# Query and key rotation by transfers instead of matrix products, a query product moved forward, and small edits at gates, reciprocals and the end

## The chip, the cores and the metric

One core of one Trainium2 chip runs the whole kernel. The metric is the device time of one execution in microseconds (us); the time before is the median of 3 runs. The granted clock of TensorE is 1.00 (2.4 GHz) in nearly the whole span.

## The reference, cut to what matters

512 tokens of width 1024 pass through two blocks of one kind ("block1", depth 2) and one of another kind. All is float32. In a block of the first kind:

```python
h = rms_norm(x, norm_mix_w[i])
proj = jnp.einsum("bld,de->ble", h, w_in[i])
q, k, v, z, xbc_raw, dt_raw = jnp.split(proj, split_at, axis=-1)
q = rms_norm(q.reshape(b, l, 8, 64), q_norm_w[i])
k = rms_norm(k.reshape(b, l, 2, 64), k_norm_w[i])
q = axial_rope(q, cos_r, sin_r, cos_c, sin_c)
k = axial_rope(k, cos_r, sin_r, cos_c, sin_c)
attn_out = blocked_gqa(q, k, v)
ssd_out = ssd_mixer(z, xbc_raw, dt_raw, ...)
x = x + jnp.einsum("ble,ed->bld", jnp.concatenate([attn_out, ssd_out], -1), w_out[i])
```

`axial_rope` splits the 64 channels of a head into a row half and a column half, and each half into two pieces of 16, `x1` and `x2`, and gives `x1*cos - x2*sin` and `x2*cos + x1*sin`. The SSD mixer runs a centred convolution of five taps and a silu over `xbc`, then a chunked scan (4 chunks of 128 tokens, 2 directions), a gate with silu(z) and a group norm. A gated feed-forward layer follows each block. The third block has a recurrence with heads, a gated linear recurrence (`lru`) with a gelu gate, a long convolution, and another feed-forward layer; a last rms norm ends the program.

## The kernel before, in words

**Tiling.** Activations lie with channels on the 128 partitions and the 512 tokens along the free dimension, 8 tiles for a width of 1024. A weight product of one 128-column tile is 8 rows of the contraction. Each float32 operand is split into a high and a low part in fp32r, and a row is three products (lines 1343 to 1345). The weights come as one stream in the order in which they are used: SyncE loads a slot into `WR` (4 buffers, line 2481), ScalarE rounds it to `WHI` (line 1614), VectorE takes the rest as `WLO` (line 1994). Small products (transposes, attention, scan) are plain float32 products and show as two records each for 512 columns.

**Order.** A planner (`class Order`) writes one list of steps before the build; each engine runs its own steps of that list in that order, so an instruction that waits holds up what stands behind it on its engine. The planner keeps a clock of its own: `TIMES` gives an assumed cost per step, a weight product advances the clock, and chains (generators) wait in it until steps are added (`added`) or assumed done (`until`), or until a PSUM bank is free (`room`). A chain's steps are put between the rows of the weight products when they are due.

**block1.** After the z product come the products dt (column 2192), v (640) and then `IN_ORDER` = (4, 10, 11, 12, 13, 14, 15, 0, 1, 2, 3, 16, 17): keys; x (10 to 13) and B (14, 15) for the scan; the four query tiles; C (16, 17). Each of keys and queries is evicted to a slot of `RQ` (line 1696). Every `xbc` tile goes through `conv` (VectorE, line 2083) and a silu after every second one (line 1686). Chains beside the products:

- `rotated(l, t)`, t = 0 for keys, 1 to 4 for queries: `rsq` squares on ScalarE (1707); `rmm` sums them on TensorE (1385); `rroot` gives 1/sqrt on ScalarE (1593, 1594); `rnorm` scales on VectorE (2097); `rturn` multiplies with a constant matrix on TensorE (1395) that exchanges the pieces and changes a sign; for the keys this is done twice, with a plain product (1393) beside it, since each of the two key heads has to stand on both halves of the partitions (`KD`); `rope` takes `x*cos + turned*sin` on VectorE (2109 to 2111). A rotation waits for the one before.
- `attention`: 16 pairs of heads and token chunks (`pair_chunk`), below called attention chunks, four to each query tile; each starts when keys and its query tile are rotated, at least `pace` (4.0 during the products) apart in the planner's clock. A chunk has a product with the keys (`qk`, 1493), two row maxima (2242), two exps (1775), two reciprocals (`nrm`, 2247), two scalings (`prs`, 1781), eight transposes (1305), two evictions (1788), 16 products with v (`pv`, 1508), a cast and a subtraction (1793, 2252).
- `ssd_states` before, and `ssd_decay`, `ssd_scores`, `ssd_rows` after the last silu (the step `xsilu` 7): products for running sums (1442), scores (1432), then per token chunk c: `dec` (1453), `dexp` (1744), `w` (2196), `xc` (2189), `yt` (1473), `ytc` (1753), `yb`, `gyb`, `gsq` (1758), `zout` (2227). The step `ya` on VectorE (2205) starts the gate of a chunk. When chunk 3 is through, the gated result is transposed back (`zT`).
- After that, four products with `w_out` run together: rows 0 to 3 need attention, rows 4 to 7 the transposed scan result.

**lru.** In block 2, `lru_in(j)` runs two products and, for j of at least 2, lets the planner wait until `yl` of j - 2 is added before the gelu eviction. The gate products (`gates`, 1572) wait for a convolution on VectorE (2361).

**The end.** After the last weight product: add to x (2069, 2071), square (1637), add to the accumulator (2015), a product with ones (1379), 1/sqrt (1593, 1594), then the tiles of x are scaled: 5 on VectorE (2035) and 3, whose norm weight ScalarE has multiplied in before (`xweight`), on GpSimd (`xroot`, 2452). SyncE stores each (2503).

```python
    def rotated(self, l, t):
        if t > 0:
            yield from self.until(("rope", l, t - 1, 1 if t == 1 else 0))
        yield self.add("rsq", l, t)
        ...
        yield self.add("rnorm", l, t)
        for i in range(2 if t == 0 else 1):
            ...
            yield self.add("rturn", l, t, i)
            done = self.add("rope", l, t, i)
```

## Time and profile before

| | us |
|---|---|
| runs shown, median of 3 | 2763.72 (2761.19 to 2764.48) |
| the profiled execution's own time | 2760.8 |
| its span | 2758.8 |
| TensorE busy | 2707.8 (98%) |
| VectorE busy | 1524.2 (55%) |
| ScalarE busy | 1150.2 (42%) |
| GpSimd busy | 22.7 (1%) |
| share of TensorE in the chain that ended last | 91% |

A busy TensorE is one with a product in its pipeline; a full stream of weight products starts one every 0.23 us, so a row takes 0.68 us and a product of 8 rows 5.4 us. The window from 45 to 162.7 us is the product stretch of the first block1, 162.7 to 237.3 us its tail, where scan and attention run without weight products but for the last few us. The second block1 has the same two from 664 to 786.4 and from 786.4 to 861.

### The profile page before, as it was taken

The page shows a single profiled execution, that of the slowest core. Times are in us where ns is not written, and L with a number is a line of the kernel's source. Part 1 is how long each engine was busy: PE and PEld are TensorE (multiplying, and loading weights), DVE is VectorE, ACT ScalarE, POOL GpSimd, SP SyncE. Part 2 cuts the span into 40 slices and gives each one's busy share as a digit, 9 for nine tenths or more (in the row PEclk, how much of TensorE's full clock was granted, in tenths as well). Part 3 has the DMA queues.
Part 4 walks back from the last instruction along what each step waited for, and adds up shares of the span by engine and source line. Part 5 has one row for each costly group of instructions (what it writes and reads, how often), then busy time and mean ns, then how long its engine had stood idle before and what let it go on. Part 6 is the DMA issues. An engine that isn't in the chain of part 4 may idle for free.

```text
span 2758.8 us, 33405 instructions
## 1 busy us (share of the span) xinstructions
PE 2707.8 (98%) x13734; PEld 2183.5 (79%) x13734; DVE 1524.2 (55%) x2136; ACT 1150.2 (42%) x1678; POOL 22.7 (1%) x40
## 2 busy tenths in 40 slices
PE   8998999999999999999999999999999999999997
PEld 6767888888767888888888887777777888888886
DVE  5775444345776444344443446878889854544433
ACT  5585322224584322233222234455587452422221
POOL 0000000000000000000000000000000000000000
PEclk9999999999999999999999999999999999999999
DMA  5102323233201332232332342221223322322231
GB/s 207 61 21 69 108 99 100 92 99 135 69 20 64 113 100 97 94 98 93 100 99 94 95 136 92 69 69 62 81 75 105 123 99 92 99 97 95 96 95 62
DMA packets 72071, 253.42 MB, mean 92 GB/s; under 512 B 8304, under 2 KB 9456, under 8 KB 71536
## 3 DMA queue, kind: packets, MB, share of 16 engines
q1 hardware_dynamic: 69408, 238.19, 26.5%
q0 software_dynamic: 2512, 13.11, 1.3%
q8 instruction: 109, 1.79, 0.3%
q14 instruction: 42, 0.34, 0.0%
HBM read 242.87 MB, written 8.39 MB: 91 GB/s over the span
## 4 chain that ended last, share of the span: by engine, by line
PE 91%; ACT 5%; DVE 3%; issue 1%; DMA 0%; SPq 0%; DVEq 0%; ACTq 0%
PE PS L1343 27%; PE PS L1344 27%; PE PS L1345 27%; PE PS L1526 1%; PE PS L1305 1%; PE PS L1363 1%; PE PS L1364 1%; PE PS L1365 1%; PE PS L1493 1%; ACT PT L1788 0%; PE PS L1508 0%; ACT WHI L1614 0%; ACT DE L1744 0%; PE PS L1424 0%; ACT L1604 0%
## 5 line engine op out<-in xcount | busy, mean ns | idle before, releaser
L1343 PE MATMUL PS<-HHI,WHI 128*128 128x512 f32 x2288 | 915.6, 400 | 0.0
L1345 PE MATMUL PS<-HHI,WLO 128*128 128x512 f32 x2288 | 891.6, 390 | 0.0
L1344 PE MATMUL PS<-HLO,WHI 128*128 128x512 f32 x2288 | 891.2, 390 | 0.0
L1994 DVE TENSOR_TENSOR WLO<-WR,WHI 128x1024 fp32r<-128x1024 f32 (+2 forms) x446 | 536.3, 1204 | 555.8 <-ACT WHI L1614 552.3
L1614 ACT CAST WHI<-WR 128x1024 fp32r<-128x1024 f32 (+2 forms) x446 | 457.4, 1026 | 349.1 <-PE PS L1345 332.5
L1343 PEld LDWEIGHTS PS<-HHI,WHI 128*128 128x128 f32 x2288 | 429.6, 188 | 97.6 <-issue 8.8
L1344 PEld LDWEIGHTS PS<-HLO,WHI 128*128 128x128 f32 x2288 | 429.9, 188 | 92.1 <-issue 7.0
L1345 PEld LDWEIGHTS PS<-HHI,WLO 128*128 128x128 f32 x2288 | 429.5, 188 | 89.9
L1343 PE MATMUL PS<-FHI,WHI 128*128 128x512 f32 x704 | 273.9, 389 | 0.0
L1344 PE MATMUL PS<-FLO,WHI 128*128 128x512 f32 x704 | 273.9, 389 | 0.0
L1345 PE MATMUL PS<-FHI,WLO 128*128 128x512 f32 x704 | 273.9, 389 | 0.0
L1670 ACT CAST FHI<-SQF 128x512 fp32r<-128x512 f32 x88 | 54.6, 620 | 330.3 <-DVE SQF L2055 330.3
L1666 ACT ACTIVATE SQF<-SQF 128x512 f32<-128x512 f32 x88 | 55.6, 632 | 313.9 <-DVE SQF L2048 313.9
L2354 DVE SCALAR_TENSOR_TENSOR CVA<-CU,VEC,CVA 128x511 f32<-128x511 f32 (+14 forms) x240 | 163.6, 728 | 1.9 <-ACT CVA L1886 1.9
L1343 PEld LDWEIGHTS PS<-FHI,WHI 128*128 128x128 f32 x704 | 132.2, 188 | 27.6
L1345 PEld LDWEIGHTS PS<-FHI,WLO 128*128 128x128 f32 x704 | 132.2, 188 | 27.5
L1344 PEld LDWEIGHTS PS<-FLO,WHI 128*128 128x128 f32 x704 | 132.2, 188 | 27.1
L2055 DVE TENSOR_TENSOR SQF<-SQF,PS 128x512 f32<-128x512 f32 x88 | 60.5, 688 | 164.8 <-PE PS L1345 162.0
L2048 DVE TENSOR_TENSOR SQF<-PS,RS 128x512 f32<-128x512 f32 x88 | 60.8, 691 | 142.8 <-PE PS L1345 142.8
L1343 PE MATMUL PS<-YHI,WHI 128*128 128x512 f32 x320 | 127.8, 399 | 2.1 <-DVE WLO L1994 2.1
L1345 PE MATMUL PS<-YHI,WLO 128*128 128x512 f32 x320 | 124.7, 390 | 0.0
L1344 PE MATMUL PS<-YLO,WHI 128*128 128x512 f32 x320 | 124.5, 389 | 0.0
(329 smaller groups left out, 2555.5 us busy)
## 6 DMA issues: line engine op xcount, KB each, us to landing
WR<-in_stream SPq DMA_DIRECT2D x413, 512.0 KB, 3.4
WR<-in_stream SPq DMA_DIRECT2D x32, 384.0 KB, 3.1
xkeep<-X POOLq DMA_DIRECT2D x3, 2048.0 KB, 8.8
X<-xkeep POOLq DMA_DIRECT2D x24, 256.0 KB, 5.0
X<-in_xin SPq DMA_DIRECT2D x8, 256.0 KB, 7.4
out<-X SPq DMA_DIRECT2D x8, 256.0 KB, 2.1
GW<-in_gates SPq DMA_DIRECT2D x8, 128.0 KB, 3.4
RT<-in_rope SPq DMA_DIRECT2D x2, 320.0 KB, 5.6
```

The costliest lines, as they stand in the source:

```text
L1305: t = e.transpose(out[:, i * P:(i + 1) * P], src, ident)
L1343: e.matmul(out, hi[:, i, :], xhi, start=first, stop=False)
L1344: e.matmul(out, hi[:, i, :], xlo, start=False, stop=False)
L1345: t = e.matmul(out, lo[:, i, :], xhi, start=False, stop=final)
L1363: e.matmul(out, xhi, hi[:, i, :], start=r == 0, stop=False)
L1614: e.copy(hi, raw).then_inc(S["act_high"], 1)
L1666: e.activation(SQ[:, j % 2, :], SQ[:, j % 2, :], ACT.Silu).then_inc(S["act_silu"], 1)
L1670: e.copy(FHI[:, j, :], HF[:, j % 2, :]).then_inc(S["act_xhigh"], 1)
L1994: e.tensor_tensor(lo, raw, hi.bitcast(F32), ALU.subtract).then_inc(S["dve_low"], 1)
L2048: e.tensor_tensor(SQ[:, j % 2, :], PS[o.bank["gate", f, j]][:, :], RS[:, :], ALU.mult).then_inc(S["dve_gs"], 1)
L2055: e.tensor_tensor(HF[:, j % 2, :], SQ[:, j % 2, :], PS[o.bank["up", f, j]][:, :], ALU.mult).then_inc(S["dve_mul"], 1)
L2354: e.scalar_tensor_tensor(acc[:, s:T], CU[:, j, 0:T - s], vec("cvw", 8 * (TAPS - 1 - s) + j), acc[:, s:T], ALU.mult, ALU.add).then_inc(S["d ...
```

## The change

- The rotation's matrix products go. The host permutes the columns of `w_in` for queries and keys (`PAIRED`), so that in each head the partner of channel d stands 32 partitions away. `swap` copies, by four DMAs of 32 partitions each on SyncE's queue, the raw tile into `ROT` with the halves exchanged. `rcs` (VectorE) forms `raw*w*cos` and `swapped*w'*sin` (the sign is in the table), `rope` adds them and multiplies by the inverse root. For the keys the result goes to a slot of `RQ`, and `kdup` writes it four times into `KD` by DMAs on SyncE's queue.
- `rsq` and `rmm` of a rotation no longer wait for the rotation before.
- `IN_ORDER` becomes (4, 0, 10, 11, 12, 13, 14, 15, 1, 2, 3, 16, 17).
- One reciprocal of two columns for each attention chunk; both scalings wait for it, and it waits for both exps.
- `ya` runs on GpSimd.
- The gelu eviction of `lru_in` becomes a chain (`lru_gate`), and the planner goes on to the next product.
- At the end, the product with ones is taken in two parts: over the accumulator up to tile 6 while the last weight products run (`sumx`), and over the last square (`sum`). `xweight` and `xroot` go; VectorE scales all eight tiles, stored in order.

In the diff below, cut to its core, the step `ya` stands in the function of GpSimd (before, in that of VectorE), `swap` and `kdup` in that of SyncE.

```diff
-IN_ORDER = (4, 10, 11, 12, 13, 14, 15, 0, 1, 2, 3, 16, 17)
+IN_ORDER = (4, 0, 10, 11, 12, 13, 14, 15, 1, 2, 3, 16, 17)
...
+    def sum_ahead(self):
+        yield ("acc", 8, DT - 2)
+        yield from self.room()
+        self.take(("sum", 8, 0), "side")
+        self.add("sumx", 8)
...
     def rotated(self, l, t):
+        self.spawn(self.turned(l, t))
         if t > 0:
-            yield from self.until(("rope", l, t - 1, 1 if t == 1 else 0))
+            yield from self.until(("rmm", l, t - 1))
         yield self.add("rsq", l, t)
         yield from self.room()
         self.take(("rmm", l, t), "side")
         yield self.add("rmm", l, t)
+        if t > 0:
+            yield from self.until(("rope", l, t - 1))
         root = self.add("rroot", l, t)
         self.free(("rmm", l, t), ("act_rooted", root))
         yield root
-        yield self.add("rnorm", l, t)
-        for i in range(2 if t == 0 else 1):
-            yield from self.room(2 if t == 0 else 1)
...
+        yield from self.until(("rcs", l, t))
+        yield self.add("rope", l, t)
+        if t == 0:
+            yield self.add("kdup", l)
+
+    def turned(self, l, t):
+        if t > 1:
+            yield from self.added(("rope", l, t - 2))
+        yield self.add("swap", l, t)
+        yield 1.2
+        if t > 0:
+            yield from self.added(("rope", l, t - 1))
+        self.add("rcs", l, t)
...
         yield exp
-        yield self.add("nrm", l, i)
+        if i % 2:
+            self.add("nrm", l, i // 2)
+        yield from self.until(("nrm", l, i // 2))
         yield self.add("prs", l, i)
...
+        self.spawn(self.lru_gate(j))
+
+    def lru_gate(self, j):
         if j >= 2:
-            self.run(lambda: ("yl", j - 2) in self.n)
+            yield from self.added(("yl", j - 2))
+        yield 0.0
         self.free(("lg", j), ("act_gelu", self.add("gelu", j)))
...
+            elif kind == "sumx":
...
+                q.wait_ge(S["dve_acc"], n["acc", m, DT - 2])
...
+                e.matmul(PS[o.bank["sum", m, 0]][:, :], ONES, ACC[:, :], start=True, stop=False)
+            elif kind == "sum" and a[0] == 8:
...
+                q.wait_ge(S["act_square"], n["sq", m, DT - 1])
+                e.matmul(PS[o.bank["sum", m, 0]][:, :], ONES, SQ[:, (DT - 1) % 2, :], start=False, stop=True).then_inc(S["pe_ones"], 1)
...
+            elif kind == "rcs":
+                q.wait_ge(s_rope, 32 * (l + 1))
+                q.wait_ge(S["act_raw"], n["raw", l, 2 + t])
+                q.wait_ge(s_turn[t % 2], 64 * ((3 - t % 2) * l + t // 2 + 1))
...
+                e.scalar_tensor_tensor(SGB[:, 2, :], RQ[:, (2 + t) % 4, :], w[:, 0:1], COS[:, :], ALU.mult, ALU.mult)
+                e.scalar_tensor_tensor(SGB[:, 3, :], ROT[:, t % 2, :], w[:, 1:2], SIN[:, :], ALU.mult, ALU.mult).then_inc(S["dve_rcs"], 1)
+            elif kind == "rope":
...
+                settle(e.tensor_tensor(SGB[:, 2, :], SGB[:, 2, :], SGB[:, 3, :], ALU.add))
+                q.wait_ge(S["act_rooted"], n["rroot", l, t])
+                e.tensor_tensor(dst, SGB[:, 2, :], RRS[:, :], ALU.mult).then_inc(S["dve_rope"], 1)
...
+            elif kind == "ya":
...
+                q.wait_ge(S["dve_xtd"], n["xtd", l, 0])
+                q.wait_ge(S["act_xta"], n["xta", l, 3])
+                if c >= 2:
+                    q.wait_ge(S["dve_zout"], n["zout", l, c - 2])
+                else:
+                    q.wait_ge(S["pe_st"], n["st", l, 2, 1])
+                e.tensor_tensor(by_head(YA[:, :]), by_head(XST[:, c, :]), heads_by(col(l, "dsk", 0, 8)), ALU.mult).then_inc(S["pool_ya"], 1)
...
+            elif kind == "swap":
+                q.wait_ge(S["act_raw"], n["raw", l, 2 + t])
+                if t > 1:
+                    q.wait_ge(S["dve_rope"], n["rope", l, t - 2])
+                for i in range(0, P, 64):
+                    e.dma_start(ROT[i:i + 32, t % 2, :], RQ[i + 32:i + 64, (2 + t) % 4, :]).then_inc(s_turn[t % 2], 16)
+                    e.dma_start(ROT[i + 32:i + 64, t % 2, :], RQ[i:i + 32, (2 + t) % 4, :]).then_inc(s_turn[t % 2], 16)
+            elif kind == "kdup":
+                q.wait_ge(S["dve_rope"], n["rope", l, 0])
+                for g in range(2):
+                    for half in (slice(0, 64), slice(64, P)):
+                        e.dma_start(KD[half, g, :], RQ[64 * g:64 * g + 64, 2, :]).then_inc(s_keys, 16)
```

## Rows read from the trace of the kernel before

**Rows 1.** The page, busy time and share of the span by engine.

```profile
PE 2707.8 (98%) x13734; PEld 2183.5 (79%) x13734; DVE 1524.2 (55%) x2136; ACT 1150.2 (42%) x1678; POOL 22.7 (1%) x40
```

**Rows 2.** Busy time by stretch: length, PE, PEld, DVE, ACT, POOL, clock, DMA share, GB/s.

```profile
45.00:162.70 117.70, 116.04 (x574) 85.77 (x572) 80.05 (x128) 67.63 (x117) 0.00 (x0) 1.00 0.21 68
162.70:237.30 74.60, 63.57 (x758) 47.81 (x759) 57.56 (x126) 58.49 (x142) 0.56 (x1) 1.00 0.04 12
...
786.40:861.00 74.60, 64.72 (x738) 48.65 (x739) 57.97 (x127) 59.04 (x144) 0.55 (x1) 1.00 0.04 12
...
2743.50:2758.80 15.30, 1.12 (x2) 0.30 (x2) 8.49 (x8) 3.23 (x4) 5.09 (x3) 0.67 0.36 137
```

**Rows 3.** The line 1395 from 40 to 260 us, two records to a product.

```profile
L1395 PE MATMUL PS<-RQ,RT x12: 590/592/697, 65.7 to 156.6; 128*128 128x512 f32 x12
```

**Rows 4.** The chain that ended last, in order of time: start, us, what.

```profile
64.96 0.86 PE PS L1393 x2
...
92.25 0.87 PE PS L1305 x8
...
114.82 1.06 PE PS L1493 x4
...
136.44 1.02 PE PS L1508 x16
```

**Rows 5.** Groups of PE from 162.7 to 237.3 us: count, busy, mean, idle before.

```profile
L1508 PE MATMUL PS<-PT,V 128*64 128x128 f32 x176 | 11.8, 277 | 3.5 <-ACT PT L1788 3.5
L1493 PE MATMUL PS<-KD,Q 64*128 64x512 f32 x32 | 9.4, 641 | 0.0
```

**Rows 6.** Groups of DVE from 162.7 to 237.3 us.

```profile
L2242 DVE TENSOR_REDUCE NM<-PS 128x1 f32<-128x512 f32 x18 | 11.5, 679 | 0.7 <-PE PS L1493 0.7
...
L2252 DVE TENSOR_TENSOR YLO<-PS,YHI 128x128 fp32r<-128x128 f32 x13 | 3.6, 285 | 10.3 <-ACT YHI L1793 10.3
...
L2205 DVE TENSOR_TENSOR YA<-XBC,VEC 128x512 f32<-128x512 f32 x4 | 2.7, 678 | 0.0
...
L2247 DVE RECIPROCAL RIN<-RSM 128x1 f32<-128x1 f32 x22 | 2.6, 150 | 0.4 <-ACT RQ L1775 0.3
```

**Rows 7.** Timeline of PE from 205 to 240 us.

```profile
218.38 1.17 PE L1453 MATMUL PS<-RUNB,RUNA 32*128 32x128 f32 x32
...
237.29 0.60 PE L1305 MATMUL PS<-CON,Z 128*128 128x128 f32 x4
```

**Rows 8.** Groups of ACT from 60 to 115 us.

```profile
L1614 ACT CAST WHI<-WR 128x1024 fp32r<-128x1024 f32 x8 | 8.4, 1049 | 17.7 <-PE PS L1345 17.7
...
L1686 ACT ACT_TABLE_LOAD x1 | 1.3, 1283 | 0.0
```

**Rows 9.** DMA issues with KB each and median us to landing; then SP's longest wait.

```profile
X<-xkeep POOLq DMA_DIRECT2D x24, 256.0 KB, 5.0
...
out<-X SPq DMA_DIRECT2D x8, 256.0 KB, 2.1
...
SPq L2481 <- DVE WLO L1994: 2527.6, 440, 87.1
```

**Rows 10.** The line 2035, alone from 1318.9 us, beside GpSimd at the end.

```profile
L2035 DVE SCALAR_TENSOR_TENSOR X<-X,VEC,ACC x8: 745/746/746, 1318.9 to 1395.1; 128x512 f32<-128x512 f32 x8
L2035 DVE SCALAR_TENSOR_TENSOR X<-X,VEC,RS x5: 740/1745/1752, 2748.9 to 2754.6; 128x512 f32<-128x512 f32 x5
```

**Rows 11.** Timeline of the end, from 2743.4 us.

```profile
2745.64 0.69 DVE L2015 TENSOR_TENSOR ACC<-ACC,SQF 128x512 f32<-128x512 f32 x1 [0.69 <-ACT SQF L1637]
...
2746.39 1.12 PE L1379 MATMUL PS<-ACC,CON 128*128 128x512 f32 x2 [2.90 <-DVE ACC L2015]
...
2748.93 6.42 DVE L2035 SCALAR_TENSOR_TENSOR X<-X,VEC,RS 128x512 f32<-128x512 f32 x5 [2.60 <-ACT RS L1594]
2749.05 5.09 POOL L2452 TENSOR_TENSOR X<-X,RS 128x512 f32<-128x512 f32 x3 [574.72 <-ACT RS L1594]
```

**Rows 12.** Timeline of PE in the lru stage, the gate product that waits.

```profile
2013.09 1.98 PE L1572 MATMUL PS<-XB,GW 128*128 128x512 f32 x4 [3.43 <-DVE XB L2361]
```

More of the change, by code:

```diff
@@ L204, in __init__ @@
         self.steps, self.n, self.count = [], {}, {}
-        self.now, self.end, self.engine_end = 0.0, {}, {"pe": 0.0, "dve": 0.0, "act": 0.0, "pool": 0.0}
+        self.now, self.end, self.engine_end = 0.0, {}, {"pe": 0.0, "dve": 0.0, "act": 0.0, "pool": 0.0, "sp": 0.0}
         self.functions = None
@@ L431, in add_to_x @@
         self.new_x(m, j)
[L432 to L434 removed]
+        if m == 8 and j == DT - 2:
+            self.spawn(self.sum_ahead())
     def ffn(self, f, gate, up, down, i, up0):
@@ L528, in attention @@
         for u in range(NH // 2 * CH):
-            yield from self.until(("rope", l, 0, 1), ("rope", l, 1 + u // 4, 0))
+            yield from self.until(("kdup", l), ("rope", l, 1 + u // 4))
             if u >= 1:
@@ L619, in ssd_decay @@
     def ssd_decay(self, l):
-        yield from self.until(("rope", l, 4, 0))
+        yield from self.until(("rope", l, 4))
         self.add("limits", l)
@@ L718, in raw @@
             self.product(("raw", l, t), ("H", 2 * l), "w_in", l, c0)
-            first = {4: ("dtT", l), 5: ("vT", l), 6: ("rope", l, 0, 1)}.get(t)
+            first = {4: ("dtT", l), 5: ("vT", l), 6: ("kdup", l)}.get(t)
             if first:
@@ L1064, in whole @@
         self.block2()
-        self.spawn(self.mean_square(8))
         self.run()
+        self.add("sum", 8)
+        self.free(("sum", 8, 0), ("act_rooted", self.add("root", 8)))
         for j in range(DT):
-            kind = "xroot" if j in SHARED else "xscale"
-            self.x[kind, 8, j] = self.x_now[j]
-            self.x["store", j] = self.x_now[j] = self.add(kind, 8, j)
-        for j in (3, 0, 4, 1, 5, 6, 2, 7):
+            self.x["xscale", 8, j] = self.x_now[j]
+            self.x["store", j] = self.x_now[j] = self.add("xscale", 8, j)
             self.add("store", j)
@@ L1290, in x_ready @@
             q.wait_ge(S["dve_add"], n[made])
-        elif kind == "xweight":
-            q.wait_ge(S["act_xweight"], n[made])
-        elif kind == "xroot":
-            q.wait_ge(S["pool_xroot"], n[made])
         else:
@@ L1860, in scalar_engine @@
                 t.then_inc(S["act_half"], 1)
-            elif kind == "xweight":
-                m, j = a
-                x_ready(q, o.x[step])
-                e.activation(X[:, j, :], X[:, j, :], ACT.Copy, scale=norm_weight(m, j)).then_inc(S["act_xweight"], 1)
             elif kind == "rosq":
@@ L2447, in gpsimd_engine @@
                 e.dma_start(X[:, j, :], xkeep[:, j * T:(j + 1) * T]).then_inc(s_back[j], 16)
-            elif kind == "xroot":
-                m, j = a
-                x_ready(q, o.x[step])
-                q.wait_ge(S["act_rooted"], n["root", m])
-                e.tensor_tensor(X[:, j, :], X[:, j, :], RS[:, :], ALU.mult).then_inc(S["pool_xroot"], 1)
+            elif kind == "ya":
+                l, c = a
+                YA = YAS[c % 2]
+                q.wait_ge(s_con, 32)
+                done(q, ("xbc", l, 7))
+                q.wait_ge(S["dve_xtd"], n["xtd", l, 0])
[5 more added lines that the diff above has]
+                e.tensor_tensor(by_head(YA[:, :]), by_head(XST[:, c, :]), heads_by(col(l, "dsk", 0, 8)), ALU.mult).then_inc(S["pool_ya"], 1)
             elif kind == "rf":
@@ L2511, in build @@
         block.gpsimd(gpsimd_engine)
+PAIRED = np.concatenate([np.arange(16) + k for k in (0, 32, 16, 48)])
 def shape_constants():
@@ L2558 @@
         w = w[r0 * P:(r0 + nr) * P, c0:c0 + ncol]
+        if name == "w_in" and c0 < 640:
+            w = w.reshape(-1, 2, 64)[:, :, PAIRED].reshape(-1, ncol)
         pieces.append(w.reshape(nr, P, ncol).transpose(1, 0, 2).reshape(-1))
@@ L2574 @@
         put(("nmix", l), a["norm_mix_w"][l])
-        put(("qn", l), np.concatenate([a["q_norm_w"][l]] * 2))
-        put(("kn", l), np.concatenate([a["k_norm_w"][l]] * 2))
+        for key in ("q", "k"):
+            w = a[f"{key}_norm_w"][l][PAIRED]
+            put((f"{key}n", l), np.concatenate([w, w, np.roll(w, 32), np.roll(w, 32)]))
         put(("cw", l), a["conv_w"][l])
```

132 lines of the change are left out of this document (45 added, 87 removed), and 4 rows, old and new, of the table TIMES.

## The prediction

> **What bounds the kernel now.** I read the busy shares first: TensorE is busy for 2707.8 of 2758.8 us [rows 1], so 51.0 us of the span are left in which it is idle, and every other engine has time to spare on average. So there are only two ways to win: take products off TensorE, or shorten its 51.0 us of idle time. The table by stretch says where that idle time is [rows 2]. In the product stretch of block1 it is 1.7 of 117.7 us: TensorE is the bound there, and whatever leaves it shortens the stretch. In the two tails it is 74.6 - 63.6 = 11.0 and 74.6 - 64.7 = 9.9 us, while VectorE (57.6) and ScalarE (58.5) are busy for almost as long as TensorE: there nothing is the bound alone, and chains of waits set the pace. At the end it is 14.2 us. One product of the lru stage waits 3.4 us for VectorE [rows 12]. These three places and the start hold nearly all of it.
>
> **Products taken out.** In a block1 line 1395 has 12 records, which is 6 products [rows 3], and line 1393 two more for the keys: 8 products of 128x512. In the chain such a product takes 0.86 us [rows 4]. 8 x 0.86 = 6.9 us for each block, 13.8 us in all, nearly all of them in the stretch without idle time, so they count in full.
>
> **The query moved forward.** Moving a product changes no work. It changes when attention starts: now the first attention chunk starts at 114.8 us [rows 4], after the first query has come behind the six x and B products. With the query right behind the keys, the four chunks of query 0 can run during those six products (33 us); the next query stands where it stood. One chunk costs TensorE 1.06 (keys) + 0.87 (transposes) + 1.02 (v) = 2.95 us, say 3.0 [rows 4]. From 114.8 to 162.7 us 8 chunks started, the other 8 in the tail (32 records of line 1493, four to a chunk), where 11 were finished (176 records of line 1508, 16 to a chunk) [rows 5]: on average 9.5 chunks lie in the tail. I take it that 6 of these leave it, four by the move and two because queries 1 to 3 find attention free at once; 3.5 remain.
>
> *Product stretch:* -6.9 + 6 x 3.0 = +11.1 us: 162.7 becomes 173.8.
>
> *Tail:* VectorE is busy for 57.6 us in it [rows 2]. Of this attention has 11.5 + 2.6 + 3.6 = 17.7 us (maxima, reciprocals, subtractions) [rows 6], or 1.86 for each of 9.5 chunks; the scan has 39.9. With 3.5 chunks: 39.9 + 6.5 = 46.4. To this come VectorE's idle 17.0 us; 10.3 of them stand ahead of the subtraction that waits for attention's cast [rows 6]. If that part falls with the chunks (10.3 x 3.5 / 9.5 = 3.8), 10.5 remain, and the tail is 56.9 us. The first transpose of the scan's result, now at 237.3 [rows 7], then comes at 230.7: 6.6 us won, and 6 us with a little left for plans that don't fit. So **each block1 gains 6.0 us**, less than the 6.9 of its products: the moved work leaves a stretch where it was partly covered by waits for one where it is not. Two blocks: -12.0. Bounds: if the tail's idle time falls to 8, -9 a block; if it stays at 17.0, 173.8 + 63.4 = 237.2 and nothing is won.
>
> **What the move costs elsewhere.** Exps now fall between the silus of x and B. A change of ScalarE's table takes 1.28 us [rows 8]; three silu pairs with exps on both sides need up to 4 more, 5.1 us a block. What hides them is ScalarE's idle time in that stretch: 17.7 us ahead of its casts, where it waited for TensorE [rows 8]. In the tail ScalarE spends 58.5 us on 9.5 chunks and the scan [rows 2], at most 6 us a chunk and, with the scan's part off, by my estimate 4; four chunks so put 16 us there too, so the cover is nearly used up, but the stretch also grows by 12 us. I cost it at nothing; if the cover is gone, at most 5.1 us a block.
>
> **Transfers of the rotation.** 5 x 4 + 4 = 24 DMAs a block on SyncE's queue. No row shows a transfer within SBUF; the nearest land after 2.1 us (a store) and 5.0 us (a return from `xkeep` on another queue) [rows 9]. I take 2.1 plus the issues of four, about 3.5 us, since the queue is the store's and the size is smaller. Behind `swap` and `kdup` stand weight loads on the same queue; SyncE waits for VectorE for 2527.6 us in total ahead of them [rows 9], a load is asked for four slots before its use, and a wait of a few us there costs nothing. `rcs` waits on VectorE with casts of weights and `conv` behind it; these have three slots (16 us) ahead of TensorE. The chain of a rotation has lost two steps on TensorE and gained a transfer that runs beside the square root, so it is not longer. At nothing; bounds 0 and (5.0 - 2.1) x 2 = 6 us for the first rotation of both blocks, for which `qk` of chunk 0 waits on TensorE's own queue.
>
> **VectorE's own savings** are 3 operations of the keys' rotation, 16 of 32 reciprocals at 0.15, and `ya`, 4 x 0.68 a block [rows 6]: in the tail about 1.2 + 2.7 us.
>
> **ya on GpSimd.** At the end GpSimd takes 5.09 / 3 = 1.70 us for a tile [rows 11], and a VectorE operation beside it 1.745 instead of 0.745 us [rows 10]. So each `ya` may cost VectorE 1.0 us and save it 0.68: +1.3 us a block if every one meets such an operation, -2.7 if none does. With the reciprocals this is about nothing, and I leave it out of the sum; ends -8 and +3 us. The Trainium skill has a rule that speaks against this step (SBUF — State Buffer, Who interferes with whom): VectorE and GpSimd share one read port, and an operation of VectorE with two inputs in SBUF and one of GpSimd that reads SBUF exclude each other for a whole instruction. The rows agree (1.745 for 1.70); by that rule alone, met by every `ya`, the sum would be 2 x 1.3 = 2.6 us worse; by a GpSimd that disturbs nobody, 5.4 us better.
>
> **Gates.** The planner no longer stands still for `yl`, so rows of weight products come ahead of the gate product that waits 3.43 us [rows 12]. Half of it: -1.7; bounds -3.4 and 0, below nothing too, since the gelu moves behind other work: +1.
>
> **The end.** The sum over tile 7 alone saves the accumulation, 2745.64 to 2746.39: -0.75 [rows 11]. Its first part is a further product in the last weight products, +0.86 [rows 4]. The scaling took 6.42 us [rows 11]; eight operations on VectorE alone take at most 8 x 0.745 = 5.96 [rows 10], and operations of this kind follow each other a little closer than that: 5.4. -1.0. Together -0.9; ends -0.4 and -1.5.
>
> **Sum.** -12.0 - 1.7 - 0.9 = -14.6 us against the profiled execution's own 2760.8: 2746.2. The median of the runs is 2.9 us higher, 2763.7, and the result is a median too: **2749.1 us**. A difference under 0.2% (5.5 us) can't be told from none.
>
> **Rivals.**
> A. *The tails shrink more* (0.17). VectorE's idle time in them falls to 8 us and `ya` and the reciprocals count. Block1 gains 9 to 12: -18 to -24, with the rest -21 to -27: about 2740. For it: waits for attention's cast are the largest single wait. Against: when attention is gone, nothing fills the scan's own waits.
> B. *The moved work finds no gap to close* (0.14). The tail keeps its 17 us of idle time on VectorE, a block gains nothing, and 2.6 us remain: 2761. For it: TensorE's idle time in the tail is only 11 us; the removed products are then paid for by new idle time.
> C. *The rotation is late* (0.07). Transfer, table loads and an in-order wait at the first `qk` cost 3 to 6 us a block: 2749.1 + 9 = 2758.
> D. *Slower* (0.10): the scan's chain alone. From the decay products of chunk 3 to the transpose of the result it takes 237.3 - 218.4 = 18.9 us, of which 12 up to the end of `yt`; if the four chunks hardly overlap, the tail is 4 x 12 + 7 (end) + 9 (start) = 64 us however little attention is in it. If then attention has left it nearly whole (7.5 chunks, stretch to 178.3), a block ends at 242.3, 5.0 later: +10.0 - 2.6 = +7.4, 2771. A block is even at a tail of 60.3 us (with the 1.3 us that the rest wins for it), and the whole is slower by more than 5.5 us from 63 us on. Against: `DE` has two buffers, so the decays of one chunk can be made beside the products of the one before.
> My forecast has 0.52: -9 to -19.
>
> **Range and chances.** Forecast's own range 2744 to 2755. Reaching to most of A, to B and C: 2738 to 2762; outside are D and the far end of A, 0.10 + 0.05. Faster by over 0.2%: forecast, A and a third of C: 0.72; same: B and the rest of C, 0.18; slower: D, 0.10.
>
> **What would show it.** TensorE busy about 2707.8 - 13.8 + 0.9 = 2694.9. First `qk` near 75 us and four chunks before 112; the last weight product of the stretch near 174 instead of 163; the tail near 57 us, with 11 to 14 us of idle time on TensorE. VectorE idle ahead of `rcs` for the transfer under 1 us each. `ya` 1.7 us on GpSimd, with VectorE operations of 1.7 us beside it. At the end eight scalings in 5.4 to 6 us. Wrong would be: a tail over 60 us (D), an idle TensorE between 62 and 112 us (C), or a stretch that isn't longer at all because attention was not moved.

## The result and the profile after

| | before | after |
|---|---|---|
| median of the runs, us | 2763.63 (2761.19 to 2764.48, 4 runs) | 2736.82 (2736.66 to 2737.71, 4 runs) |
| profiled execution's own time / span | 2760.8 / 2758.8 | 2736.9 / 2735.1 |

The ratio is 0.9905 (0.9893 to 0.9917): faster by 26.8 us in the medians and by 23.9 in the two profiled executions. The forecast was 2749.1 us, its range 2738 to 2762: the sign was right, the size was little more than half of what came, and the result lies 1.2 us below the range.

The page of the kernel after, busy time by engine, to stand beside [rows 1]:

```profile
span 2735.1 us, 33373 instructions
...
PE 2695.2 (99%) x13704; PEld 2176.0 (80%) x13704; DVE 1511.9 (55%) x2092; ACT 1158.2 (42%) x1683; POOL 25.7 (1%) x45
```

TensorE is busy for 2695.2 us (forecast 2694.9): the work taken out is as counted. The span fell by 23.7, so 11.1 us came out of TensorE's idle time, of which the forecast had expected almost nothing. The table by stretch says where; columns as in [rows 2]:

```profile
core 0: us, PE busy (x) PEld busy (x) DVE busy (x) ACT busy (x) POOL busy (x), PEclk, DMA share, GB/s
...
44.00:162.80 118.80, 115.52 (x656) 86.53 (x656) 81.72 (x129) 80.09 (x137) 2.58 (x3) 1.00 0.28 85
162.80:226.10 63.30, 57.18 (x663) 43.51 (x660) 50.65 (x102) 50.40 (x127) 2.09 (x2) 1.00 0.03 9
...
776.60:840.00 63.40, 57.34 (x664) 43.42 (x661) 50.69 (x102) 50.47 (x128) 2.09 (x2) 1.00 0.03 10
```

In the tails TensorE is idle for 63.3 - 57.2 = 6.1 us, twice; before, 11.0 and 9.9. In the stretch its idle time rose from 1.7 to 3.3 us.

From here on a block1 is measured by three marks in the timeline of TensorE: the first product of `PS<-SD,CON`, the scan's first score product (`PS<-XBC`, end of the product stretch) and the first transpose of the scan's result (`PS<-CON,Z`, end of the tail).

| us | before | after |
|---|---|---|
| first block1: marks | 53.2, 162.7, 237.3 | 52.3, 162.8, 225.5 |
| stretch / tail | 109.5 / 74.6 | 110.5 / 62.7 |
| second block1: marks | 676.9, 786.5, 859.0 | 665.8, 776.6, 839.3 |
| stretch / tail | 109.6 / 72.5 | 110.8 / 62.7 |

The blocks give -10.9 and -8.6 us; -0.9 lies ahead of the first mark, +0.7 between the blocks, -4.0 behind the second (lru stage and end): -23.7. Where gates or end alone were undone and the steps of a block1 stayed as they are, its stretch took 109.8 to 110.7 us and its tail 62.6 to 62.7, so a stretch is known to about 1 us, a tail much better.

What stands in a tail, the groups on PE from 162.8 to 225.5 us (before: [rows 5]):

```profile
line engine op names shapes xcount | busy us, mean ns | idle before us <-releasers
L1521 PE MATMUL PS<-PT,V 128*64 128x128 f32 x160 | 10.7, 277 | 2.1 <-ACT PT L1803 1.9
L1506 PE MATMUL PS<-KD,Q 64*128 64x512 f32 x28 | 8.8, 640 | 0.1
...
L1454 PE MATMUL PS<-CON,SD 128*32 128x128 f32 x68 | 2.2, 274 | 0.0
```

28 records of scores are seven chunks, 160 with V ten: one chunk fewer than before in each, where the forecast had six fewer. What did leave as well are running sums of the scan (`PS<-CON,SD`): the kernel before has 128 records in its first tail, this one 64 (the 68 shown take in four that began ahead of the mark); the other 64, about 2 us, now stand in the stretch.

Taken between the marks, the books of the first block close. In the tail TensorE's busy time fell from 63.6 to 56.6 us and its idle time from 11.0 to 6.1. In the stretch it is busy for 108.4 us in both kernels: the 7.0 us of work that came in from the tail fill the room that the eight products left, and its idle time grew by 1.0 us. That is 7.0 + 4.9 - 1.0 = 10.9 us. In the second block the tail lost 6.1 us of work and 3.7 of idle time, the stretch 1.0 of work, and 2.2 us of idle time came to the stretch: 8.6.

And on VectorE, same stretch:

```profile
L2243 DVE TENSOR_REDUCE NM<-PS 128x1 f32<-128x512 f32 x14 | 9.0, 681 | 0.1
...
L2215 DVE TENSOR_TENSOR YA<-YA,YB 128x512 f32<-128x512 f32 x6 | 4.5, 750 | 0.2
...
L2253 DVE TENSOR_TENSOR YLO<-PS,YHI 128x128 fp32r<-128x128 f32 x10 | 2.7, 282 | 7.7 <-ACT YHI L1808 7.7
...
L2248 DVE RECIPROCAL RIN<-RSM 128x2 f32<-128x2 f32 x9 | 1.3, 154 | 0.0
```

VectorE's busy time fell from 57.6 to 50.7, not to 46.4, and its largest wait, for attention's cast, from 10.3 to 7.7 [rows 6], not to 3.8.

One difference of order stands out in a tail. Ahead of the fourth decay product (`PS<-RUNB,RUNA`) the timeline of TensorE before reads:

```profile
210.86 0.66 PE L1305 MATMUL PS<-CON,SGB 128*128 128x128 f32 x4
211.45 1.13 PE L1493 MATMUL PS<-KD,Q 64*128 64x512 f32 x4
212.51 0.66 PE L1305 MATMUL PS<-CON,YT 128*128 128x128 f32 x4
213.00 0.60 PE L1305 MATMUL PS<-CON,PR 128*128 128x128 f32 x4
213.53 1.09 PE L1508 MATMUL PS<-PT,V 128*64 128x128 f32 x16
214.56 0.66 PE L1305 MATMUL PS<-CON,PR 128*128 128x128 f32 x4
216.19 0.66 PE L1305 MATMUL PS<-CON,RQ 128*128 128x128 f32 x4 [0.97 <-ACT RQ L1781]
216.77 1.09 PE L1508 MATMUL PS<-PT,V 128*64 128x128 f32 x16
217.80 0.66 PE L1305 MATMUL PS<-CON,RQ 128*128 128x128 f32 x4
218.38 0.84 PE L1453 MATMUL PS<-RUNB,RUNA 32*128 32x128 f32 x20
```

and after:

```profile
206.38 0.39 PE L1485 MATMUL PS<-DE,XCB 128*64 128x128 f32 x4
206.70 0.66 PE L1318 MATMUL PS<-CON,PR 128*128 128x128 f32 x4
207.38 1.17 PE L1465 MATMUL PS<-RUNB,RUNA 32*128 32x128 f32 x32
```

After, it comes one group behind the products of the third chunk's scan; before, the nine groups shown stand between, 7.5 us. From the last decay product to the end of the tail it is 18.9 us before and 18.1 after (16.8 and 18.0 in the second block), and this product stands 55.7 - 44.6 = 11.1 us nearer to the end of the stretch. That the tail ends sooner because of it is a guess from two kernels; the section on what holds the tail puts it beside the others.

The parts with a small price. The transfers of the rotation, and `ya` in the timeline of GpSimd:

```profile
ROT<-RQ SPq DMA_DIRECT2D x40, 64.0 KB, 2.0
...
KD<-RQ SPq DMA_DIRECT2D x8, 128.0 KB, 3.9
```

```profile
156.45 2.04 POOL L2460 TENSOR_TENSOR YA<-XBC,VEC 128x512 f32<-128x512 f32 x2 [12.19 <-PE PS L1436]
197.15 1.04 POOL L2460 TENSOR_TENSOR YA<-XBC,VEC 128x512 f32<-128x512 f32 x1 [38.66 <-DVE Z L2228]
207.04 1.04 POOL L2460 TENSOR_TENSOR YA<-XBC,VEC 128x512 f32<-128x512 f32 x1 [8.85 <-DVE Z L2228]
```

Who waits for the transfers (total us, times, longest):

```profile
DVE SGB L2112 <- DMA ROT<-RQ: 11.7, 8, 3.4
PEld PS L1506 <- DMA KD<-RQ: 2.9, 2, 1.6
PE PS L1506 <- DMA KD<-RQ: 2.1, 2, 1.2
```

VectorE waits for swapped tiles eight times, up to 3.4 us each, and the trace lists nobody who waits for the operations behind these waits; TensorE waits 2.1 us in both blocks together for the keys' copies, ahead of the first scores. And the end, against [rows 11]:

```profile
2724.36 1.29 PE L1388 MATMUL PS<-SQF,CON 128*128 128x512 f32 x2 [2.17 <-ACT SQF L1650]
...
2727.07 5.39 DVE L2046 SCALAR_TENSOR_TENSOR X<-X,VEC,RS 128x512 f32<-128x512 f32 x8 [3.42 <-ACT RS L1607]
```

Eight scalings in 5.39 us where 6.42 stood.

### The profile page after: what moved, and what is told of

It reads as the page before. It is cut to its first block, busy times and chain, and to the rows that moved or that the text cites. A ratio compares the mean times of both kernels' runs of the same rounds, so it can differ in the third digit from the quotient of the medians.

```text
span 2735.1 us, 33373 instructions
## 1 busy us (share of the span) xinstructions
PE 2695.2 (99%) x13704; PEld 2176.0 (80%) x13704; DVE 1511.9 (55%) x2092; ACT 1158.2 (42%) x1683; POOL 25.7 (1%) x45
## 4 chain that ended last, share of the span: by engine, by line
PE 91%; ACT 5%; DVE 3%; issue 1%; DMA 1%; SPq 0%; DVEq 0%; ACTq 0%
PE PS L1356 27%; PE PS L1358 27%; PE PS L1357 27%; PE PS L1539 1%; PE PS L1318 1%; PE PS L1506 1%; PE PS L1376 1%; PE PS L1377 1%; PE PS L1378 1%; PE PS L1521 1%; ACT WHI L1627 1%; ACT PT L1803 1%; DVE WLO L2005 1%; ACT DE L1759 0%; PE PS L1485 0%
```

## The experiments

The median of the kernel before lay between 2761.7 and 2763.6 us beside them. Marks, stretches and tails are those of the table above.

### The parts, one at a time

**Rotation alone**, on the kernel before (`swap`, `rcs`, `rope`, `kdup`, squares freed; order, reciprocals, `ya`, gates and end as before).

```diff
-            yield from self.until(("rope", l, t - 1, 1 if t == 1 else 0))
+            yield from self.until(("rmm", l, t - 1))
...
-            yield self.add("rturn", l, t, i)
...
+        self.add("swap", l, t)
...
+        self.add("rcs", l, t)
```

> The kernel before with the rotation by transfers (and the squares freed from the rotation before), and nothing else of the change. Theory 1, only the 16 products count: about 13.8 us faster than before (2749.8), the product stretch of a block1 6.9 us shorter (110.8), its tail as before (74.6 and 72.5). Theory 2, the shorter chain of a rotation also lets the scan and attention of the tail start earlier: tails under 70 us and more than 18 us in all. Theory 3, the rotation gives less than its products, since VectorE and TensorE wait for the transfers: under 10 us.

2758.6 us, ratio 0.9984 (0.9975 to 0.9994): 4.3 us, though the eight products are gone. Marks 52.4, 158.2, 234.8 and 674.4, 780.1, 856.8: the stretch is 3.7 and 3.9 us shorter, the tail 2.0 and 4.2 longer. The time is theory 3's, but not for its reason alone. The plan moved: nine chunks of scores are left in a tail instead of eight, and all running sums stand in the stretch. And at seven places ahead of the end the granted clock falls to 1.2 GHz, where the kernel before has one fall; among them

```profile
core 0: us, PE busy (x) PEld busy (x) DVE busy (x) ACT busy (x) POOL busy (x), PEclk, DMA share, GB/s
149.00:155.00 6.00, 5.43 (x72) 3.40 (x76) 3.51 (x9) 5.82 (x8) 0.00 (x0) 0.72 0.00 0
203.00:209.00 6.00, 5.83 (x61) 3.86 (x62) 0.99 (x6) 5.94 (x17) 0.00 (x0) 0.72 0.01 3
224.00:230.00 6.00, 4.72 (x41) 4.14 (x42) 3.96 (x9) 1.53 (x2) 0.00 (x0) 0.72 0.00 0
```

so TensorE goes at 1.2 GHz for 3.4 us of each. Ahead of the three it was busy for 6.7 of 9, 6.0 of 8 and 4.9 of 8 us. In the tails of the changed kernel, and of the kernel before, the clock never falls.

**Order alone**, on the kernel before.

```diff
-IN_ORDER = (4, 10, 11, 12, 13, 14, 15, 0, 1, 2, 3, 16, 17)
+IN_ORDER = (4, 0, 10, 11, 12, 13, 14, 15, 1, 2, 3, 16, 17)
```

> The kernel before with the new order of the input products and nothing else. Theory 1 (the prediction's): six attention chunks leave the tail, the product stretch grows by 18 us and the tail shrinks by as much: 0 to 2 us from before. Theory 2, one chunk or so moves, since ScalarE is the limit in the first stretch, and the tail loses waits: 3 to 8 us faster.

2777.1 us, ratio 1.0051 (1.0036 to 1.0066): **slower by 14 us**. The tails take 81.4 and 82.3 us. The last query's rotation sum comes at 166.6 us, behind the end of the stretch (150.0 before), and the first decay product at 192.1 (175.4): in the plan the scan's decay steps (`ssd_decay`) start only when the last rotation is done. Both theories had the sign wrong.

**Order undone** in the changed kernel, the same line the other way round.

> The changed kernel with the old order of the input products. If the order brings what the two blocks gained beyond their products (4.2 us), it takes about 2741 us. If the order is worth nothing, 2737. If it is worth more than that because other parts lean on it (a tail over 70 us), 2745 or more.

2754.2 us, ratio 0.9969 (0.9958 to 0.9980): 17.3 us slower than the change. Tails of 74.7 and 73.0 us; 36 records of scores and 208 with V in the first, nine and thirteen chunks against seven and ten. So the order gives 17 us with the other parts in place and costs 14 on the kernel before. Of the 17.3, 4.1 lie behind the second block, where this execution has a wait of 3.3 us ahead of a product with `YHI` and a fall of the clock at 875.6 us that the changed kernel lacks.

**Order and freed squares**, on the kernel before, the rotation still by products.

```diff
-            yield from self.until(("rope", l, t - 1, 1 if t == 1 else 0))
+            yield from self.until(("rmm", l, t - 1))
```

> The kernel before with the new order of the input products, and with the squares of a query no longer waiting for the rotation of the one before, but with the rotation still made by products on TensorE. Theory (the line of rotations is what made the order cost 14 us): the last rotation sum comes 10 us or more before the 166.6 us of the order alone, the tails fall from 81.4 to 72 to 76 us, time 2757 to 2766 us. Rival (the round trip through TensorE and VectorE for the turned query is the brake, not the squares): last rotation sum after 160 us, tails over 79 us, time 2772 to 2778 us.

2768.1 us, ratio 1.0017 (1.0007 to 1.0026). The last rotation sum falls from 166.6 to 142.6 us and 9 of the 14 us are back. Of the two, the theory holds, with tails of 74.9 us and a time 2 us past its range: the line of rotations is the larger part of what made the order dear. **Squares in line again**, in the changed kernel:

```diff
-                yield from self.until(("rmm", l, t - 1))
+                yield from self.until(("rope", l, t - 1))
```

> The changed kernel, but the squares of a query wait again until the rotation of the one before is finished (before, every rotation stood in such a line). Theory (the order pays only because the five rotations no longer stand in line): the last query's rotation sum, at 136.3 us with the change, comes later, by some 2 us for each of the last three queries, the scan's first decay product moves from 172.4 to about 178, and the two tails grow from 62.7 to 66 to 69 us: 2743 to 2750 us. Rival (the transfers alone shorten a rotation enough, the place of the squares doesn't matter): first decay product within 1 us, tails under 63.5 us, time 2736 to 2739 us.

2748.6 us, 11.8 slower than the change. The theory's time came, its way only in part: the last rotation sum comes at 140.1 us, 3.8 later (2.6 against the first mark), the first tail grows to 72.2 and the second stays at 62.3 behind a stretch 2.8 longer. In both the clock is at 1.2 GHz again, for 13.6 and 6.8 us, so up to 6.8 of the 9.5 us in the first tail can be the clock:

```profile
163.50:235.70 72.20, 61.22 (x655) 46.41 (x656) 52.21 (x103) 52.42 (x128) 4.85 (x2) 0.91 0.03 9
...
789.60:851.90 62.30, 55.25 (x579) 42.68 (x576) 50.15 (x100) 48.92 (x122) 2.46 (x2) 0.95 0.03 6
```

**Products back**: the changed kernel with eight rotation sums repeated in each block, at the same places.

```diff
+                for _ in range(4 if t == 0 else 1):
+                    e.matmul(PS[o.bank[step]][:, :], BONES, SGB[:, 0, :], start=True, stop=True)
```

> The changed kernel with 8 float32 products of 128x512 put back in each block1, as repeats of the sum of squares (4 for the keys, 1 for each query); no step of the plan moves. Theory 1, a product taken from TensorE counts in full: 16 x 0.86 = +13.8 us (2750.6), stretches 6.9 us longer, tails at 62.7. Theory 2, part of it is absorbed where TensorE waits for ScalarE or VectorE in the stretch: +7 to +12.

2749.4 us, +12.5: the stretches are 5.9 and 5.6 us longer, the tails 62.7 as they were; 1.1 us lie ahead of the first mark, where this execution has a fall of the clock at 24.3 us. Eight products are worth 6 us a block, all in the stretch. Of the change's gain in a block, 10.9 and 8.6, that leaves 5 and 3. Most of it is TensorE's idle time, 4.9 and 3.7 us less in the tails against 1.0 and 2.2 more in the stretches; 1 to 1.5 us a block stay unassigned.

**Reciprocals, `ya`, gates and end undone**, one each, in the changed kernel.

```diff
-        if i % 2:
-            self.add("nrm", l, i // 2)
-        yield from self.until(("nrm", l, i // 2))
+        yield self.add("nrm", l, i)
```

> The changed kernel with one reciprocal for each head. It changes VectorE's load by 16 operations of 0.15 us a block and lets the first head's scaling go before the second exp. Theory 1, VectorE's load counts in the tail: +1 to +3 us in all. Theory 2, worth nothing or against the change: -1 to +1. If the clock of TensorE falls to 1.2 GHz somewhere in the tail, as it did in the two runs of the rotation and of the order alone, up to 1.7 us more for each fall of 3.4 us.

> The changed kernel with ya back on VectorE. Theory 1, ya on GpSimd takes 2.7 us off VectorE in a tail where VectorE sets the pace, and all of it counts: +2 to +5 us. Theory 2, it is covered by VectorE's idle time in the tail: within 1 us.

> The changed kernel with the planner waiting for yl before the gelu eviction again. Between the sixth branch of the long convolution and the product of the mean the changed kernel gained 3.6 us against the kernel before. If that is this edit, +3 to +4 us (2740.4), with a wait of about 3.4 us of a gate product for VectorE; if it came from another shift in time, 0.

> The changed kernel with the end of the kernel before (one product with ones after the last accumulation, three tiles on GpSimd). By the two traces the end gained 1.1 us net of the product that it puts into the last weight products: +1 us; by the prediction's sum +0.9. If the further product is covered, +2.

Reciprocals: 2744.0, +7.1, where at most 3 was expected: the stretches are longer by 2.9 and 2.0 us, the tails by 1.0 and -0.4. 16 operations of 0.15 us can't be that. The plan moved: six chunks of scores are left in a tail instead of seven, so one more (3 us) stands in each stretch, and the tail doesn't get shorter for it. That this is the cost was not tried by itself. `ya` back on VectorE (its step moved as it stands, with its wait on `st`): 2737.5, +0.7 with tails 1.1 longer. Gates (`self.run(lambda: ("yl", j - 2) in self.n)` again): 2742.6, but only +2.7 in the profiled execution's span: 3.6 us behind the second block, where the wait of 3.4 us ahead of the gate products is back, less 1.0 us of a shorter second stretch. The profiled execution has a mean granted clock of 0.998, the other three 0.997, 0.997 and 0.996. End with `xweight`, `xroot` and one product with ones: 2737.6, +0.7.

Undone singly (for the rotation only its products put back) the parts cost 17.3 + 12.5 + 7.1 + 5.8 + 0.7 + 0.7 = 44 us, together 27. They don't add up. Order and reciprocals move the steps of the other parts in the plan, as the chunk counts show.

### Would a stronger dose give more?

**Second query two products sooner**, and **two queries behind the keys**, in the changed kernel:

```diff
-IN_ORDER = (4, 0, 10, 11, 12, 13, 14, 15, 1, 2, 3, 16, 17)
+IN_ORDER = (4, 0, 10, 11, 12, 13, 1, 14, 15, 2, 3, 16, 17)
```

> The changed kernel with the second query two products sooner: keys, a query, four of x, a query, B, the two last. Theory 1 (tails are held by the scan, whose work can start no earlier when x comes later): attention in the tail falls by up to one or two chunks, but the first decay product comes no sooner and the stretch grows by as much: 2735 to 2742 us. Theory 2 (attention in the tail is what holds it): each tail falls by 2 to 4 us with a stretch less than 1 us longer, 2729 to 2734 us.

```diff
-IN_ORDER = (4, 0, 10, 11, 12, 13, 14, 15, 1, 2, 3, 16, 17)
+IN_ORDER = (4, 0, 1, 10, 11, 12, 13, 14, 15, 2, 3, 16, 17)
```

> The changed kernel with two queries behind the keys, then x and B: keys, two queries, six of x and B, two queries, C. The forecast's mechanism (attention leaves the tail and fills the stretch) would show here more strongly: stretch longer by some 6 us, tail shorter by more. Theory (what counts is when the last rotation lets the decay products start, not how much attention is left): the last rotation sum stays within 3 us of 136.3, tails within 2 us of 62.7, time 2735 to 2741 us. Rival (more attention ahead of the tail shortens it further): tails 58 to 60 us, stretches within 1 us, time 2729 to 2734 us.

2746.8 and 2748.4 us, both some 10 to 12 slower than the change; none of the theories had a loss of this size. With the second query two products sooner, six chunks of scores are left in a tail; the stretches are 0.9 and 1.8 us longer, the tails 68.2 and 65.7, of which the clock (at 1.2 GHz for 6.8 and 3.4 us) can be 3.4 and 1.7. With two queries first, five chunks of scores are left in the first tail instead of seven. The stretches are 116.4 us (+5.9 and +5.6, two chunks of 3 us each), the tails 64.7 and 61.1 (in each TensorE goes at 1.2 GHz for 3.4 us, worth 1.7 at most). Here the forecast's mechanism is seen in pure form, and only its first half works: what attention takes from the tail it adds to the stretch in full, and the tail gives almost nothing back. The change's own order is the best of the four tried with its other parts.

### What holds the tail

Three kernels keep the order of the steps and leave out part of the work of some.

**Attention thinned** in the changed kernel, and in the kernel before: the last 7 of 16 chunks handle 128 of the 512 keys.

```diff
-                for k in range(CH):
+                last = 0 if u >= 9 else CH - 1
+                for k in range(last + 1):
...
+                w = P if i >= 18 else T
+                e.activation(PRS[PR_OF[i]][:, 0:w], PS[o.bank["qk", l, i]][:, 0:w], ACT.Exp, bias=NM[:, k:k + 1],
```

> The changed kernel with the same order of instructions, but the last 7 of the 16 attention chunks handle 128 of the 512 keys (a quarter of the columns in the scores, maxima, exps, scalings, transposes and products with V); the rest of their sums is left out. That takes some 19 us of TensorE's work, 14 of ScalarE's and 6 of VectorE's out of a tail. Theory (the tail of 62.7 us is the length of the scan's own chain, attention fits beside it): tails 57 to 62 us, 2724 to 2736 us. Rival (attention and the scan together fill the engines, and the tail is their sum): tails 43 to 50 us, 2697 to 2712 us.

> The same cut of the last 7 chunks in the kernel before, whose tails take 74.6 and 72.5 us. Theory (before, the tail was longer than the scan's chain because chunks and the late last rotation stood in its way): tails fall to 58 to 64 us, close to those of the changed kernel with the same cut, 2735 to 2750 us. Rival (even before, the scan's chain from the last rotation on set the tail): tails stay above 70 us, 2755 to 2762 us.

2725.0 and 2749.7 us. The tails, after and before, from the last score mark to the first transpose:

```profile
162.60:219.20 56.60, 47.37 (x532) 36.98 (x529) 44.83 (x102) 37.68 (x127) 2.08 (x2) 0.91 0.03 9
769.50:826.80 57.30, 48.11 (x532) 37.22 (x529) 45.05 (x102) 37.72 (x127) 2.09 (x2) 0.91 0.03 10
```

```profile
162.10:231.30 69.20, 55.38 (x632) 42.36 (x633) 51.99 (x126) 45.53 (x142) 0.56 (x1) 0.90 0.04 13
780.50:846.20 65.70, 52.67 (x599) 40.55 (x600) 51.43 (x126) 45.31 (x142) 0.55 (x1) 0.95 0.04 13
```

In the changed kernel ScalarE loses 12.7 us of work in a tail and TensorE 9.2 in the first (19 was expected; the granted clock of 0.91 hides part), yet the tail loses only 6.1 and 5.4, to 56.6 and 57.3. Both the time and the tails are the theory's, or just under. Even with all of the 9% of the clock given back (5 us) the rival's 43 to 50 is not reached. In the kernel before it loses 5.4 and 6.8 and stays at 69.2 and 65.7, between the two expectations. Attention's work is thus worth about the same in both, and the distance between the two kernels is left whole: 12.6 and 8.4 us, as against 11.9 and 9.8 unthinned. In the thinned pair the last decay product comes 37.6 and 39.0 us behind the start of the tail after, 49.6 and 47.1 before: 12.0 and 8.1 us apart, again nearly the distance of the tails.

**Scan thinned** in the changed kernel: one direction is left out of the products with the decays, and its masks cover a quarter of their columns.

```diff
-                    for d in range(2):
+                    for d in range(1):
...
-                decays = DE[:, c % 2, 2 * d + g, :, :]
+                w = 1 if d else 4
+                decays = DE[:, c % 2, 2 * d + g, 0:w, :]
```

> The changed kernel with the same order of instructions, but with one direction of the scan left out of the products with the decays (64 records of 0.28 us fewer in a tail, 6.2 us of TensorE) and two of four masks of a chunk applied to a quarter of their columns (some 4 us of VectorE in a tail). Attention is whole. Theory (the scan's chain is the tail): all of 1.6 us of products and about 1 us of masks a chunk stand in it, tails fall by 7 to 10 us to 53 to 56, 2715 to 2722 us. Rival (TensorE's and ScalarE's sum of work is the tail): tails fall by 3 to 6 us, 2725 to 2731 us.

2730.5 us, tails of 59.8 twice, 2.9 shorter: below the theory (7 to 10) and just under its rival (3 to 6), whose time, 2725 to 2731, it meets. Neither attention's work nor the scan's, made smaller in place, moves a tail by more than 7 us.

**Is it the place of the last decay product?** No run moved it alone, and as a measure of the tail it fails in other kernels. With order and freed squares on the kernel before, the second tail has no fall of the clock:

```profile
790.40:865.30 74.90, 63.52 (x758) 47.90 (x759) 59.30 (x129) 57.83 (x141) 0.55 (x1) 1.00 0.04 12
```

```profile
838.43 1.17 PE L1455 MATMUL PS<-RUNB,RUNA 32*128 32x128 f32 x32 [1.88 <-ACT PT L1792]
...
841.11 1.17 PE L1455 MATMUL PS<-RUNB,RUNA 32*128 32x128 f32 x32 [0.48 <-ACT DE L1748]
```

Here the last decay product comes 50.7 us behind the end of the stretch, 5.0 sooner than in the kernel before, and the tail is 2.4 us longer, since it ends 24.2 us behind this product and not 16.8. The third decay product stands only 2.7 us ahead of the fourth. With the squares in line again the last decay product of the first tail stands where the change has it (45.2 against 44.6), and the tail takes 72.2 us, of which the clock can be 6.8. Over all kernels the end comes 16.8 to 27.0 us behind the last decay product. So an early last decay product is not enough for a short tail; what sets the idle time in a tail stays open.

## Why the prediction was right and wrong

- **Products taken out** (6.9 us a block): right in kind, a little too large. 5.9 and 5.6 measured by putting eight back; TensorE's busy time came out within 0.3 us.
- **The query moved forward** is the step that failed, and with it the two sums behind it. The prediction let 6 of 9.5 chunks leave the tail, and so the stretch grow by 11.1 us. The first chunk started at 72.6 as forecast (75) and the fourth at 94.4, but the fifth waited for the second query (127.5) and the rest followed 7 us apart instead of 6: nine by the end instead of eight, so one chunk left the tail, and the stretch grew by 1.0 and 1.2 instead of 11.1. The prediction let four early chunks come on top of an unchanged rest, without asking what paces the rest.
- **The tail as VectorE's busy time and its idle time**, 46.4 + 10.5 = 56.9: measured 62.7, with VectorE busy for 50.7 and idle for 12.0. Most of the miss is again the chunks that didn't leave. The two errors have opposite signs: a stretch 10 us too long and a tail 5.8 too short left a block gain of 6.0 where 10.9 and 8.6 came. The prediction's own sign of being wrong, a tail over 60 us, was met, though the time was better than forecast.
- **Rival D** named a tail of 64 us, 1.3 from the measured one, but that is in part luck: it has four steps of 12 us that hardly overlap, where the decay products of the changed kernel stand 9.6 us behind the start and then 3.4, 21.3 and 10.3 apart, with 18.1 to the end. D also put the end of the stretch at 178.3 and so became a loss. With D's tail and the stretch as measured a block gives 74.6 - 64 - 1.0 = 9.6 us, near what came. Tail and stretch were weighed as one case where they were two questions.
- **Why the tail fell by 12 us**: 7.0 of the first tail's 11.9 us are TensorE's work that moved into the stretch, 4.9 its idle time. Shown is that a short tail needs both the order and the rotation by transfers (76.6 us with the rotation alone, 74.9 with order and freed squares, 74.7 and 73.0 with the order undone). Why the idle time fell is not shown; the last decay product stands 11.1 us nearer to the end of the stretch, but other kernels have it early too and a long tail.
- **Clock**: nothing of it stood in the forecast, and the profile of before hardly showed it (one fall near 25 us, which some of the profiled executions have and others lack; without it the start is 0.9 us shorter). The rotation alone may lose a part of its 14 us to it; how large a part was not separated.
- **Transfers of the rotation** at nothing, bounds 0 and 6: TensorE waits 2.1 us for the keys' copies. The sign (VectorE idle under 1 us for each transfer) was missed, with eight waits of 11.7 us together, but the trace lists nobody who waits behind them.
- **ya at nothing**: right in the sum (+0.7 when undone), wrong in its price: 1.04 us instead of 1.70. Beside the `ya` at 207.04 the operation of VectorE with two inputs in SBUF takes 1.04 instead of 0.69 us, and its neighbours that read PSUM don't stretch. The Trainium skill (SBUF — State Buffer, Who interferes with whom) says that an operation of VectorE with two inputs in SBUF contends with one of GpSimd that reads SBUF, and one with at most one such input, outside the 2-port perf modes, does not. The trace agrees. Half of the `ya` run in the stretch, and one of six such operations was met in the first tail, so the 2.6 us of the case where every `ya` meets one did not come.
- **Gates** -1.7, bounds -3.4 to +1: the lru stage gave about 3.6, past the bound by a little: the waits of gate products for VectorE fell from 4.0 to 0.5 us, the whole and not half, and rows of weight products do stand in their place. Undone, it is 3.6 us there, +2.7 in the whole span and +5.8 in the medians; the last difference goes with a lower granted clock in the other executions.
- **End** -0.9: -1.1 in the trace, 0.7 by the runs.
- **Table loads** hidden: agreed, ScalarE's idle ahead of its casts between 58 and 120 us went from 17.7 to 7.5 us, and the stretch kept 1.6 us more of idle TensorE, of which about 1 is for the keys' copies.
- **The median 2.9 us above the profiled execution** was added to the sum. The profiled execution of before has a mean granted clock of 0.998. Beside the experiments, 40 different times of that kernel are on record with their clock: three at 0.998, with a mean of 2760.1 us, six at 0.997 with 2761.7, 29 at 0.996 with 2763.4, and two at 0.995 with 2764.5. The changed kernel has 0.998 in all its executions, and its median is its profiled time. So 2.9 of the 12.3 us missed are this term, and 2.9 of the 26.8 us won go with the clock by these rows. Of the other 9.4, the blocks are 7.5 (19.5 against 12.0) and the lru stage 1.9.
- **Rival A** (0.17, about 2740) came nearest. VectorE's idle time in the first tail did fall, from 17.0 to 12.0 us and not to 8; but A had it beside a stretch grown by 11.1 us, and it counted the load of `ya` and the reciprocals, of which `ya` was worth 0.7.

## What to carry to other kernels

Where a stage is a chain that shares an in-order engine with filler work, don't price it by one engine's sum of work. First ask what paces the work that is to move: here four chunks came early and the fifth still waited for the second query. Then keep two books for the engine that is the bound, the work that changes its stage and the idle time of each stage; work that only moves is paid in the other stage. A mark that moves with the time in two kernels, as the last decay product did, is a guess until a third kernel keeps to it; here others didn't. And two edits that look separate can have opposite worth alone (here +14 and -4) and pay only together; a chain that feeds the reordered work has to be shortened first. With a plan made by a greedy planner, give even a trivial edit bounds of several us on both sides: one reciprocal or two for a chunk moved 7.

## What the runs showed of the hardware

- Copies within SBUF on SyncE's queue landed 2.0 us after their issue for 64 KB and 3.9 us for 128 KB; the nearest rows before had been 2.1 and 5.0.
- GpSimd's `ya`, a product of 128x512 with one operand repeated over each head's columns, took 1.04 us. The products at the end of the kernel before took 1.70, beside VectorE operations of 0.745 us that took 1.745. An estimate from these rows: if the two engines took turns there, GpSimd's own share is 1.70 - 0.745 = 0.96 us, near the 1.04, and the 1.70 was no price of the operation alone. No run has the product at the end without its neighbour.
- TensorE's granted clock falls to 1.2 GHz inside a tail, where the engine has idled only for short times between products. In the changed kernel with thinned attention it does so at 206.5 us, for 10.2 us:

```profile
198.00:206.00 8.00, 6.31 (x85) 4.77 (x85) 7.83 (x20) 6.59 (x24) 1.04 (x1) 1.00 0.01 3
206.00:217.00 11.00, 8.52 (x49) 7.00 (x50) 7.13 (x14) 3.70 (x13) 0.00 (x0) 0.53 0.00 1
```

At the same place (195 to 204 us) the changed kernel itself has TensorE busy for 8.92 of 9 us, at a clock of 1.00. Idle time can so be paid twice, which also limits what thinning or shortening a filler can win. It need not be: the first tail of the kernel before has 11.0 us of idle time and that with single reciprocals 9.8, both at a clock of 1.00, and with order and freed squares a tail with two falls of 3.4 us each and one with none both took 74.9 us.
